# A two-block model kernel on one core: two small loads issued later, two warm-up products fewer, part of the last normalisation moved to GpSimd

## The reference

```python
def rmsnorm(x, g):
    x32 = x.astype(jnp.float32)
    y = x32 * lax.rsqrt(jnp.mean(x32 * x32, axis=-1, keepdims=True) + EPS)
    return (y * g.astype(jnp.float32)).astype(x.dtype)

h = jnp.concatenate([meta, x, ...], axis=1)        # 16 meta tokens ahead of x
a = rmsnorm(h, norm1[i]);  proj = a @ w_in[i]      # start
log_f = jax.nn.log_sigmoid(fl + forget_bias[i])    # uses forget_bias
mixed = jnp.einsum('blgc,gcd->blgd', d, pool_w)    # uses pool_w, later on
...                                                # attention, conv, LRU, MLPs
x = x + sq_relu_mlp(rmsnorm_2(x, mlp_norm[layer]), w_up[layer], w_down[layer])
return rmsnorm_2(x, final_norm)                    # end
```

## Time and profile before

| | us |
|---|---|
| median of 3 runs (lowest, highest) | 914.86 (914.39, 915.34) |
| the profiled execution, whole | 915.04 |
| its span, first to last instruction | 913.2 |
| TensorE busy | 886.5 (97%) |
| VectorE busy | 597.2 (65%) |
| ScalarE busy | 466.2 (51%) |
| GpSimd busy | 95.1 (10%) |

### The profile page before, as it was taken

One profiled execution on the slowest core, in us unless ns is written; L12 is line 12 of the kernel. 1 busy time (PEld: TensorE's weight loads), 2 busy tenths in 40 slices (PEclk: granted clock), 3 DMA queues, 4 the chain that ended last, 5 costly groups with the idle time before them and its releaser, 6 DMA issues.

```text
span 913.2 us, 19495 instructions
## 1 busy us (share of the span) xinstructions
PE 886.5 (97%) x7408; PEld 852.9 (93%) x7408; DVE 597.2 (65%) x967; ACT 466.2 (51%) x742; POOL 95.1 (10%) x149
## 2 busy tenths in 40 slices
PE   8999999999999989999999999999998999999997
PEld 8988899999999989778899999999898899999996
DVE  5676567665665676547676666668879866666665
ACT  6546765443444465337644444445786644444443
POOL 3320002000000019600100000001140100000000
PEclk9999999999999999999999999999999999999999
DMA  7532246556556647523455555554435455555551
GB/s 260 164 116 93 94 162 219 184 174 203 180 172 204 185 140 215 165 93 108 171 173 188 187 187 184 186 185 159 158 101 192 149 186 184 184 184 184 186 182 47
DMA packets 44948, 152.64 MB, mean 167 GB/s; under 512 B 5861, under 2 KB 7141, under 8 KB 44901
## 3 DMA queue, kind: packets, MB, share of 16 engines
q1 hardware_dynamic: 41184, 145.52, 48.6%
q0 software_dynamic: 2912, 5.48, 1.8%
q10 hardware_dynamic: 804, 0.98, 0.3%
HBM read 148.58 MB, written 1.05 MB: 164 GB/s over the span
## 4 chain that ended last, share of the span: by engine, by line
PE 88%; DVE 7%; ACT 2%; issue 1%; DMA 1%; SPq 0%; DVEq 0%; POOL 0%; ACTq 0%
PE bank L1239 27%; PE bank L1241 26%; PE bank L1240 26%; DVE alo L867 3%; PE bank L1588 2%; PE bank L1329 1%; DVE h L877 1%; DVE wlo L842 1%; PE bank L1274 1%; PE bank L1679 1%; PE bank L1346 1%; DMA raw<-in_slabs 1%; PE bank L1369 1%; ACT whi L467 1%; DVE sq L1172 1%
## 5 line engine op out<-in xcount | busy, mean ns | idle before, releaser
L1239 PE MATMUL bank<-ahi,whi 128*128 128x256 f32 (+1 forms) x1400 | 400.3, 286 | 5.3 <-DVE proj L886 2.9
L1241 PE MATMUL bank<-ahi,wlo 128*128 128x256 f32 (+1 forms) x1400 | 393.5, 281 | 0.0
L1240 PE MATMUL bank<-alo,whi 128*128 128x256 f32 (+1 forms) x1400 | 393.1, 281 | 0.0
L842 DVE TENSOR_TENSOR wlo<-raw,whi 128x1024 fp32r<-128x1024 f32 x273 | 333.8, 1231 | 31.2 <-ACT whi L467 30.9
L467 ACT ACTIVATE whi<-raw 128x1024 fp32r<-128x1024 f32 x273 | 282.3, 1051 | 104.4 <-PE bank L1241 99.6
L1239 PEld LDWEIGHTS bank<-ahi,whi 128*128 128x128 f32 x1400 | 263.8, 188 | 8.8 <-DVE proj L886 3.5
L1240 PEld LDWEIGHTS bank<-alo,whi 128*128 128x128 f32 x1400 | 263.9, 188 | 0.5
L1241 PEld LDWEIGHTS bank<-ahi,wlo 128*128 128x128 f32 x1400 | 264.0, 189 | 0.0
L1239 PE MATMUL bank<-hidhi,whi 128*128 128x256 f32 x704 | 198.1, 281 | 3.0 <-issue 2.1
L1240 PE MATMUL bank<-hidlo,whi 128*128 128x256 f32 x704 | 197.6, 281 | 0.0
L1241 PE MATMUL bank<-hidhi,wlo 128*128 128x256 f32 x704 | 197.5, 281 | 0.0
(11 more groups left out here) (208 smaller groups left out, 696.2 us busy)
## 6 DMA issues: line engine op xcount, KB each, us to landing
raw<-in_slabs SPq DMA_DIRECT2D x273, 512.0 KB, 3.4
shared<-zpad POOLq DMA_DIRECT2D x64, 35.5 KB, 3.1
shared<-in_convw POOLq DMA_DIRECT2D x4, 512.0 KB, 6.3
raw<-in_slabs SPq DMA_DIRECT2D x8, 128.0 KB, 5.7
vtok<-in_gatew POOLq DMA_DIRECT2D x2, 512.0 KB, 4.2
out<-y SPq DMA_DIRECT2D x4, 256.0 KB, 2.7
h<-in_xT ACTq DMA_DIRECT2D x3, 272.0 KB, 5.5
h<-in_xT SPq DMA_DIRECT2D x1, 272.0 KB, 3.2
```

The lines of the kernel that those rows point to most:

```text
L842: dve.tensor_tensor(wlo[:, n % R, :, :], raw[:, n % R, :, :], whi[:, n % R, :, :].bitcast(F32), ALU.subtract).then_inc(lo_done, 1)
L1239: pe.matmul(dst, hi, xh, start=start, stop=False, skip_group_check=True)
L1240: pe.matmul(dst, hi, xl, start=False, stop=False, skip_group_check=True)
L1241: return pe.matmul(dst, lo, xh, start=False, stop=stop, skip_group_check=True)
```

## The change

Five edits. `WARM_UP` goes from 16 to 14. The issues of `fbias` and `poolw` move on ScalarE's queue from before the first rounding to behind the last piece of the first two slabs. On GpSimd, the pair sums of the last norm become: chunks 0+1, chunks 2+3, the sum of those two (after a wait on its own sums), and chunks 4+5; TensorE sums two tiles in place of three, and still chunks 6 and 7. GpSimd also multiplies chunks 6 and 7 of `af` by `rstd` in one instruction of 512 columns, and VectorE makes three such instructions in place of four. SP stores in the order 0, 2, 6, 4, and waits for GpSimd's semaphore `last_ready` ahead of the third.

```diff
-WARM_UP = 16
+WARM_UP = 14
...
-            for c in range(0, KC, 2):
-                sp.wait_ge(fin_ready, c // 2 + 1)
+            for c in (0, 2, KC - 2, 4):
+                if c == KC - 2:
+                    sp.wait_ge(last_ready, 1)
+                else:
+                    sp.wait_ge(fin_ready, c // 2 + 1)
                 sp.dma_start(out[:, c:c + 2, :], y[:, c:c + 2, :]).then_inc(stored, 16)
...
-            pair_sums(N_FINAL, n=FINAL_PAIRS)
+            pair_sums(N_FINAL, n=2)
+            pool.wait_ge(sum_ready, KC // 2 * N_FINAL + 2)
+            pool.tensor_tensor(sq[:, 0, NMETA:], sq[:, 0, NMETA:], sq[:, 2, NMETA:], ALU.add).then_inc(sum_ready, 1)
+            pool.wait_ge(sq_ready, KC * N_FINAL + 6)
+            pool.tensor_tensor(sq[:, 4, NMETA:], sq[:, 4, NMETA:], sq[:, 5, NMETA:], ALU.add).then_inc(sum_ready, 1)
+            pool.wait_ge(rstd_ready, RS0[N_FINAL] + 1)
+            pool.wait_ge(scaled, KC - FINAL_D)
+            pool.tensor_tensor(y[:, KC - 2:, :], af[:, KC - 2:, :],
+                               rstd[:, NMETA:].rearrange("p (a t) -> p a t", a=1).broadcast_to((P, 2, SEQ)),
+                               ALU.mult).then_inc(last_ready, 1)
...
-            act.dma_start(fbias[:, :], fbias_in).then_inc(small_loaded, 16)
-            act.dma_start(poolw[:, :, :], poolw_in).then_inc(small_loaded, 16)
...
+            act.dma_start(fbias[:, :], fbias_in).then_inc(small_loaded, 16)
+            act.dma_start(poolw[:, :, :], poolw_in).then_inc(small_loaded, 16)
             split(2)
...
-            for k in range(0, KC, 2):
+            for k in range(0, KC - 2, 2):
                 dve.tensor_tensor(y[:, k:k + 2, :], af[:, k:k + 2, :],
...
-                    for j in range(FINAL_PAIRS):
-                        pe.wait_ge(sum_ready, KC // 2 * i + j + 1)
-                        pe.matmul(dst, ones[:, :], sq[:, 2 * j, lo:], start=(j == 0), stop=False)
+                    for j in range(2):
+                        pe.wait_ge(sum_ready, KC // 2 * i + 3 + j)
+                        pe.matmul(dst, ones[:, :], sq[:, 4 * j, lo:], start=(j == 0), stop=False)
```

More of the change, by code:

```diff
@@ L305, in build @@
         scaled, fin_ready, stored = sem("scaled"), sem("fin_ready"), sem("stored")
+        last_ready = sem("last_ready")
         gatew = vtok[:, :, :].rearrange("p a b -> p (a b)")[:, 0:2 * DM].rearrange("p (g c t) -> p g c t", g=2, c=KC)
```

## The result

The changed kernel takes 916.43 us (median of 20 runs, 915.87 to 917.03) against 914.85 us (20 runs, 914.39 to 915.51): ratio 1.0016, 95% interval 1.0010 to 1.0022, 1.6 us slower. The forecast was 915.7 us, with a range of 914.5 to 916.7 (915.2 to 916.4 for its own chain of causes, without the rivals).

A forecast was written before the change was run, and what follows sets the result against it. TensorE holds 88% of the chain of waits; only start and end can move. Profiled 915.04 - 0.2 (start) + 0.15 (pair sums) + 0.9 (last products) = 915.9 us, median 915.7 us, range 914.5 to 916.7.

The forecast's parts named there:

- rival (c): Start: the two issues moved on ScalarE's queue not covered, TensorE waits 0.5 us at about 15.5 us; 916.4 us, chance 0.08.
- Last products: End: GpSimd's and VectorE's products run in turn, each standing still, so stores end later; +0.9 us, bounds -0.3 and +1.5.
- The reading of the queue: End: the kernel hangs on the first store's issue plus four transfers of 0.75 us each, not on the last issue.
- Pair sums: Last norm: the sum of 4+5 starts later behind GpSimd's extra addition; +0.15 us, bounds 0 and +0.3.
- Start: Small transfers issued later let the slab piece ScalarE waits for land earlier; -0.2 us, bounds -0.3 and +0.5.
- Two warm-up products: Start: four passes go, TensorE's idle stretch grows from 0.66 to 1.1 us; no cost as long as the clock stays.
- rival (b): Start: the longer idle stretch after the warm-up lowers TensorE's clock, costing 1.7 us; 917.4 us, chance 0.07.
- Two issues on ScalarE's queue: Start: 1.07 us of issues delay slab 2's rounding, covered by 1.44 us of slack; costed at nothing, else up to 0.5 us.
- Rival (a): End: VectorE's and GpSimd's products run side by side, or GpSimd's comes first and cheap; 914.7 us median, chance 0.15.

The follow-up runs named there:

- the late memset: Kernel before plus GpSimd writing one column of an unread tile after VectorE's last product; 917.70 against 915.02 us, ratio 1.0030.
- the memset beside the products: Kernel before plus GpSimd writing 512 columns of an unread tile once the inverse root is there; 915.68 against 915.02 us, ratio 1.0007.

## Why the prediction was right, and where it was not

The time lies in the range, and the sign and the size (within 0.2%, slightly slower) are those of the forecast. Part of that is luck. At 916.43 us it lies just above the 916.4 us at which the forecast's own range ended, and right on the 916.4 us of rival (c), which did not happen: the time alone would have spoken for a cause that was not there. What set the end of the kernel, GpSimd's DRAIN, was in no term of the sum. By its steps:

- *Last products, +0.9 us forecast.* The mechanism was the one named: each engine stands still while the other's instruction with two inputs from SBUF runs. I took a value between two orders. It was GpSimd first, for which I had written 1.1 us; the first store came 1.13 us later, and the queue of stores behind it was as long as before (4.64 against 4.62 us). The reading of the queue was right too: in the twelve kernels with four stores issued without a long gap it is 4.62 to 4.65 us from the first issue to the last landing, although the last issue comes anywhere from 1.49 to 1.81 us behind the first. The other order was mis-sized: I had +0.7 to +0.9 us for VectorE first, and in the run with that order the last landing moved by 0.2 us, since two of VectorE's products got through ahead of GpSimd's. GpSimd's 512 columns took 1.26 us, not the 1.1 taken from lines 436 and 409, nor the 1.37 us that the 2x of the Trainium skill ("GPSIMD Engine Reference", its opening) would make; the truth lay between.
- *The term that was missing.* GpSimd's program needs 5.8 us to end behind its last instruction, and the whole program waits for that. Before, it was over at 910.6 us, 2.4 us ahead of SP, so no row of waits showed it. I asked what the moved product does to the stores, and not what a later last instruction does to its own engine's end. It reached 0.43 us beyond the stores in the changed kernel, and with VectorE first it reaches 2.5 us beyond them (916.2 against 913.7 us). This and the order are the 0.66 us by which the end was mis-sized (1.13 + 0.43 = 1.56 against 0.9 us); with it, the 0.06 us of the sums and nothing for the start, the sum is the 1.6 us that were measured. But the 1.13 us are not a price that could be saved by itself: in the run that stores GpSimd's chunks first SP is through 0.57 us sooner, and the end stays where GpSimd's DRAIN puts it.
- *Pair sums, +0.15 us.* TensorE's wait grew by 0.16 us as worked out, but the inverse root came only 0.06 us later: ScalarE's gains held it before, as the chain of the kernel before says (shown with the pair sums alone). The slack that I had not granted was there.
- *Start, -0.2 us.* The profile after has -0.40 us, which looks like twice the forecast. It is not shown to be the change's: with the small transfers early the same rounding lies between 8.43 and 9.13 us in single traces, with them late between 8.37 and 8.73 us. The medians of the run with this edit alone say -0.26 us with an interval of 0.8 us to either side.
- *Two warm-up products, nothing.* Right. The idle stretch ahead of TensorE's first product grew to 1.08 us as worked out, and from 7 to 16 us the granted clock was 1.00: rival (b) did not come.
- *Two issues on ScalarE's queue.* Right in its sum, wrong in its reason: I had 1.07 us of delay hidden by 1.44 us of slack, but there was no delay, since the queue issues transfers while the datapath works on what it has been handed (rows above, 9.63 to 11.64 us). Rival (c) had no ground. The reverse holds only where the datapath is idle, as in the run with more small transfers.
- Rival (a), side by side, is excluded by each run with the product.

## What to carry to other kernels

Elementwise work with two inputs from SBUF, moved from VectorE to GpSimd while VectorE has such work too, is not done beside it but in turn with it, and GpSimd's share takes longer (1.26 against 0.69 us here): before moving it look for a stretch in which the two already overlap, and read whether either is stretched. The last instruction of each engine is a cost of its own where its program's end is slow: with 5.8 us for GpSimd's, compare its last instruction plus 5.8 us with the last landing before giving it work at the end. And a landing at the start of one trace is a draw: compare it over several kernels with the same start before it is called a gain.

## What was not expected of the hardware

GpSimd's DRAIN at its program's end lasted until 5.8 us behind its last instruction in each kernel, whether that was a sum, a product or a memset of one column (5.79 us). VectorE's ended 0.05 us behind its last product in the kernel before. What GpSimd does in those 5.8 us no run here shows.

The stretch of half clock at 695.7 us is in eleven of the fourteen profiles, 3.41 us long each time, and missing in three: the changed kernel, the late memset and the memset beside the products. These three are also those whose clock rose earliest during the warm-up (at 4.1 to 4.9 us; in the eleven others at 5.6 to 6.9 us). One profile of each kernel was kept, so that it comes and goes between executions of one program is likely, not shown. It costs far less than the 1.7 us that I had worked out: from 715 to 736 us the three profiles without it gained 0.26 to 0.39 us on that of the kernel before (by the start of VectorE's split of the same slab), and the ten others with it stayed within 0.05 us.
